# Masked attention of the last four head pairs: the selection mask is added to the position table on GpSimd, and VectorE makes these pairs' weights' low parts

## What is computed

```python
# forgetting attention (heads 0 to 7)
s = einsum('bqhd,bkhd->bhqk', q, k) * HEAD_DIM**-0.5 + F[t] - F[s]      # causal
p = softmax(s); out = p @ v
# sparse attention (heads 8 to 15)
iscore = sum_h w[t,h] * relu(q_idx[t,h] . k_idx[s]) ; causal
_, sel = lax.top_k(iscore, topk)                # topk = 128
logits = einsum(q, k[sel]) * HEAD_DIM**-0.5 + rel_bias[t5_bucket(t - sel)]
logits = where(valid, logits, -inf); p = softmax(logits); out = p @ v[sel]
merged = sigmoid(gate_fox) * (y_fox @ w_branch_fox) + sigmoid(gate_dsa) * (y_dsa @ w_branch_dsa)
```

## Time and profile before

| | us |
|---|---|
| three runs | 1383.68, 1383.83, 1384.71; median 1383.83 |
| profiled execution | 1383.52, span 1381.7 |
| busy: TensorE | 1358.7 (98%) |
| busy: VectorE, ScalarE, GpSimd | 809.0 (59%), 518.1 (37%), 560.1 (41%) |
| TensorE clock granted | 0.994 |

### The profile page before, as it was taken

How to read it: one execution, slowest core, us unless ns; L and a number is a source line. 1 busy time by engine, 2 the same in 40 slices (tenths; PEclk the granted TensorE clock), 3 DMA queues, 4 the chain that set the end, 5 groups by cost and what they waited for, 6 DMA issues and landing times.

```text
span 1381.7 us, 18469 instructions
## 1 busy us (share of the span) xinstructions
PE 1358.7 (98%) x6394; PEld 1105.6 (80%) x6398; DVE 809.0 (59%) x1082; ACT 518.1 (37%) x818; POOL 560.1 (41%) x230
## 2 busy tenths in 40 slices
PE   8999999999999999999999999999999999999997
PEld 6788878888888888886777777888878888888886
DVE  4565677574765757875888865344454243352474
ACT  5333224422323323235366665322345223142233
POOL 4333434454453635324322223444425535354361
PEclk9999999999999999989999999999999999999999
DMA  7222245373665645504423133332523423224221
GB/s 247 84 80 80 85 130 156 107 213 107 198 179 154 195 124 166 163 28 131 76 77 87 52 97 88 94 105 76 153 61 107 122 76 121 78 91 121 76 92 61
DMA packets 213236, 156.68 MB, mean 113 GB/s; under 512 B 8980, under 2 KB 193680, under 8 KB 213048
## 3 DMA queue, kind: packets, MB, share of 16 engines
q1 hardware_dynamic: 212856, 155.67, 38.6%
q10 hardware_dynamic: 320, 0.22, 0.1%
HBM read 153.73 MB, written 4.74 MB: 115 GB/s over the span
## 4 chain that ended last, share of the span: by engine, by line
PE 90%; issue 3%; POOL 2%; DVE 2%; DMA 2%; ACT 1%; ACTq 0%; DVEq 0%; POOLq 0%
PE ps L565 61%; PE ps L1034 12%; PE ps L922 3%; PE ps L983 3%; POOL w_lo L528 2%; PE ps L688 2%; PE ps L899 1%; PE ps L886 1%; DMA bias_rows<-bias_rows 1%; PE ps L872 1%; PE ps L813 1%; PE ps L873 1%; PE ps L663 1%; PE ps L651 1%; ACT w_hi L1081 0%
## 5 line engine op out<-in xcount | busy, mean ns | idle before, releaser
L528 POOL TENSOR_TENSOR w_lo<-raw,w_hi 128x1024 fp32r<-128x1024 f32 x222 | 557.0, 2517 | 789.5 <-ACT w_hi L1081 789.4
L565 PE MATMUL ps<-u_hi,w_hi 128*128 128x512 f32 x984 | 395.5, 402 | 3.5 <-POOL w_lo L528 1.8
L565 PE MATMUL ps<-u_hi,w_lo 128*128 128x512 f32 x984 | 384.8, 391 | 0.0
L565 PE MATMUL ps<-u_lo,w_hi 128*128 128x512 f32 x984 | 384.5, 391 | 0.0
L1081 ACT ACTIVATE w_hi<-raw 128x1024 fp32r<-128x1024 f32 x222 | 233.0, 1053 | 283.0 <-PE ps L1034 91.0
L565 PEld LDWEIGHTS ps<-u_hi,w_hi 128*128 128x128 f32 x984 | 186.4, 189 | 42.3 <-POOL w_lo L528 3.8
L565 PEld LDWEIGHTS ps<-u_hi,w_lo 128*128 128x128 f32 x984 | 185.4, 188 | 39.7
L565 PEld LDWEIGHTS ps<-u_lo,w_hi 128*128 128x128 f32 x984 | 185.8, 189 | 36.7 <-issue 1.0
L565 PE MATMUL ps<-y_hi,w_hi 128*128 128x512 f32 x320 | 126.7, 396 | 0.2
L565 PE MATMUL ps<-y_lo,w_hi 128*128 128x512 f32 x320 | 124.6, 389 | 0.0
L565 PE MATMUL ps<-y_hi,w_lo 128*128 128x512 f32 x320 | 124.6, 389 | 0.0
(11 more groups left out here) (270 smaller groups left out, 1816.0 us busy)
## 6 DMA issues: line engine op xcount, KB each, us to landing
raw<-w_in SPq DMA_DIRECT2D x69, 512.0 KB, 3.8
raw<-w_mlp SPq DMA_DIRECT2D x64, 512.0 KB, 3.9
adaw<-w_ada SPq DMA_DIRECT2D x32, 768.0 KB, 4.6
raw<-w_up SPq DMA_DIRECT2D x32, 512.0 KB, 6.6
raw<-w_down SPq DMA_DIRECT2D x32, 512.0 KB, 6.6
raw<-w_out SPq DMA_DIRECT2D x16, 512.0 KB, 4.4
bias_rows<-bias_rows SPq DMA_DIRECT2D x4, 635.0 KB
xtok<-x SPq DMA_DIRECT2D x4, 512.0 KB, 7.9
```

The costliest lines, as they stand in the source:

```text
L528: pool.tensor_tensor(w_lo[:, s, :], raw[:, s, :], w_hi[:, s, :], ALU.subtract).then_inc(lo_ready[s], 1)
L565: last = pe.matmul(ps[0:cols, bank, :], w[:, s, c], r[:, k, :], start=(k == ks[0] and w is w_hi and r is r_hi), stop=(k == ks[-1] and w is ...
```

## The change

- Pairs 4 to 7: TensorE's third matmul of each tile (876) goes. In its place GpSimd writes table plus mask into the tile's `prob(n)`, once the transposes of the tile that used the buffer before are through, and VectorE's `logits` waits for that and takes `prob(n)` as its second input.
- GpSimd no longer makes the low parts of both slots of `st_att` blocks 6 and 7 and of the first two `st_bra` blocks. VectorE makes these eight, at n = 0 (slot 0) and n = 3 (slot 1) of pairs 4 to 7.
- ScalarE's two casts stand earlier in all pairs: the one of slot 1 before `turned_odd(p, 1)` and `coming_exp(p, 3)`, the one of slot 0 before `turned_odd(p, 3)` and `coming_exp(p, 7)`.

```diff
@@ gpsimd
+            def masked_table(p, n):
+
+                i, tile = n // 2, 8 * p + n
+                keys = (i + 1) * P
+                pool.wait_ge(sem("tab_in"), 16 * (p + 1))
+                pool.wait_ge(sem("sel_ready"), i + 1)
+                pool.wait_ge(sem("att_t"), tile + 1 - LOOK)
+                pool.tensor_tensor(prob(n), tab2[:, 2 * (p % 2) + n % 2, T - keys:T], sel[:, i, 0:keys], ALU.add
+                                   ).then_inc(sem("masks"), 1)
...
-                if st is st_bra:
-                    for s, m in bra_order:
+                if st is st_att:
+                    with pool.Fori(0, NQ + 2) as i:
+                        for s in range(st.k):
+                            lo(st, s, i)
+                    for n in range(8 * NQ):
+                        masked_table(NQ + n // 8, n % 8)
+                elif st is st_bra:
+                    for s, m in bra_order[4:]:
                         lo(st_bra, s, m)
@@ tensor, s_step
-                pe.matmul(ps[:, bank, 0:keys], q_dn[:, at, q], k_both[:, at, 0:keys], start=False, stop=False)
-                if p >= NQ:
-                    pe.wait_ge(sem("sel_ready"), i + 1)
-                    last = pe.matmul(ps[:, bank, 0:keys], identb[:], sel[:, i, 0:keys], start=False, stop=True)
-                else:
+                last = pe.matmul(ps[:, bank, 0:keys], q_dn[:, at, q], k_both[:, at, 0:keys], start=False, stop=(p >= NQ))
+                if p < NQ:
                     last = pe.matmul(ps[:, bank, keys - P:keys], identb[:], causalb[:], start=False, stop=True)
@@ scalar, loop over the pairs
+                if p + 1 < 2 * NQ:
+                    ahead(st_att, 1, p + 1)
                 turned_odd(p, 1)
                 coming_exp(p, 3)
-                if p + 1 < 2 * NQ:
-                    ahead(st_att, 1, p + 1)
-                else:
+                if p + 1 == 2 * NQ:
                     cast(st_bra, 1, 1)
                     cast(st_bra, 2, 0)
...
-                turned_odd(p, 3)
-                coming_exp(p, 7)
                 if p + 2 < 2 * NQ:
                     ahead(st_att, 0, p + 2)
                 else:
                     cast(st_bra, 0, p + 3 - 2 * NQ)
+                turned_odd(p, 3)
+                coming_exp(p, 7)
@@ vector
-                    tab = tab2[:, 2 * (p % 2) + n % 2, T - keys:T]
+                    tab = prob(n)
+                    dve.wait_ge(sem("masks"), 3 + 8 * (p - NQ) + n + 1)
...
+            def w_low(s, g):
+
+                st, i = (st_att, g) if g < 2 * NQ else (st_bra, g - 2 * NQ)
+                dve.wait_ge(hi_ready[s], st.turn(s, i) + 1)
+                dve.tensor_tensor(w_lo[:, s, :], raw[:, s, :], w_hi[:, s, :], ALU.subtract).then_inc(lo_ready[s], 1)
...
                     coming_logits(p, n)
+                    if p >= NQ and n in (0, 3):
+                        w_low(n // 3, p + 2)
```

## The result

| | median of 5 runs, us | range |
|---|---|---|
| before | 1384.71 | 1383.68 to 1385.71 |
| after | 1392.55 | 1389.88 to 1393.95 |

The ratio is 1.0057, 95% interval 1.0042 to 1.0071: the change costs 7.8 us. The profiled execution of the changed kernel has a span of 1390.4 and a granted TensorE clock of 0.990. Busy times are 1357.9 for TensorE (before 1358.7), 821.7 for VectorE (809.0) and 568.1 for GpSimd (560.1). TensorE has 4.8 us less to do and is busy for 0.8 less, which is a first hint that the matmuls that are left ran slower somewhere.

The account below looks back on a forecast made before the run. TensorE and a loop through VectorE and ScalarE bind with nearly the same period. Terms 2.7 + 0 + 0.8 + 2.3 + 3.2 = 9.0 us on 1383.52, median 0.3 above: 1392.8; own range 1388 to 1397, 8 in 10 1382.5 to 1397.

Parts of the forecast that it names:

- the loop: Path through VectorE and ScalarE from one pair's first score matmul to the next, ending in k_lows; 0.1 to 0.3 us left.
- what shortens TensorE alone gains nothing: Attention stretch: the 4.8 us of mask matmuls taken off TensorE save no time while the loop stays.
- Casts earlier, +2.7: Pairs 1 to 3: earlier slot 0 cast makes divisions wait for GpSimd's low part; 0.9 us late each, +2.7 us.
- the earlier slot 1 cast falls in idle time of ScalarE: nothing: Pairs 1 to 3: moving the slot 1 cast earlier on ScalarE costs nothing.
- Pair 4, 0: Pair 4: division free of GpSimd's low part but starts 1.05 us later; logits 5 unmoved within 0.3, so 0.
- Pair 5, +0.8: Pair 5: w_low ahead of logits 5 and mask 5 share access in turn; logits 5 from 13.8 to 14.7, +0.8 us.
- Pair 6, +2.3: Pair 6: blocked final_norm, later exponentials, divisions and w_low running into masks delay logits 5; +1.1 to +3.5, taken +2.3 us.
- mask 2 falls on the second: it waits 0.7: Tail ahead of pair 6's logits 5: mask 2 blocks the second final_norm, which waits 0.7 us.
- Last stretch, +3.2: Pair 7 to tile 6's transposes: late logits 7, w_low(1) waiting for its cast, blocked division; +2.6 to +3.9, taken +3.2 us.
- Dear masks: Rival, last four stretches: 16-bit input doubles GpSimd's mask time, about 4 x 1.3 us on top, 1398; chance 0.08.
- Columns bind after all: Rival, attention stretch: VectorE's idle time takes in everything, TensorE's 4.8 to 5.3 us go, 1378.8; chance 0.12.
- Only the cast's place costs: Rival: masks and w_low slip into idle time in pairs 4 to 7; pairs 1 to 3 lose 2.7, 1386.5; chance 0.16.

Follow-up runs that it names:

- e2: Kernel before with the mask matmuls of pairs 4 to 7 left out, so the selection isn't applied: 1382.32 us, ratio 0.9983.
- e9: Changed kernel with masked tables in spare slots, w_low, y_lows and final_norm later, slot 0 cast early from pair 3 on only: 1381.20 us, ratio 0.9974.
- e10: Kernel before with y_lows and final_norm later and the slot 0 cast early from pair 3 on; masks stay on TensorE: 1383.60 us, ratio 0.9991.
- e1: Kernel before with only ScalarE's two weight casts of each pair one step earlier: 1386.57 us, ratio 1.0012.
- e12: Changed kernel with only the low part of st_bra block 1 moved behind the last pair's last division and turned_even: 1388.06 us, ratio 1.0021.
- e11: Changed kernel with w_low moved: slot 0 behind logits 5, st_bra block 1 behind the last pair's last division: 1388.21 us, ratio 1.0026.
- e8: Kernel before with only y_lows and final_norm moved behind k_lows and logits 7: 1383.66 us, ratio 0.9989.
- e4: Changed kernel with GpSimd writing the masked tables to four spare slots instead of the buffer of the probabilities: 1387.72 us, ratio 1.0019.
- e3: Changed kernel with ScalarE's old order of casts: 1395.58 us, ratio 1.0081.
- e5: e4 with ScalarE's old order of casts and GpSimd making all low parts between the masks: 1387.81 us, ratio 1.0019.
- e7: Changed kernel with only y_lows and final_norm moved behind k_lows and logits 7: 1391.45 us, ratio 1.0043.

## Why the prediction was right

The forecast was 1392.8, the median is 1392.55. That nearness is in part luck: the sum was +9.0 and the medians show +7.8, but the kernel before had a median of 1383.83 when the forecast was made and 1384.71 beside the changed kernel. (The bounds named for the forecast's own range add up to about 1389 to 1396, not 1388 to 1397.) The windows show +7.9. Point by point:

**TensorE and the loop have nearly the same period, and the 4.8 us appear nowhere.** True of the changed kernel: in pairs 4 to 6 the chain has gaps of 1.18, 1.72 and 1.72 us ahead of the first score matmul. But "what shortens TensorE alone gains nothing" was too strong: e2 gained 2.6. I had taken the place of the loop's end as fixed, but the loop holds score matmuls too, so it should get shorter with them (not tested by itself), and the last stretch has no `k_lows`. And e9 against e10 shows that half as much as the 4.8 can be had.

**Casts earlier, +2.7.** Right in mechanism (longer divisions in pairs 1 to 3, seen in the changed kernel and in e1), mis-sized: 1.92. And the three pairs aren't alike: 1.10, 0.42 and 0.40. In pair 2 logits 5 comes 14.07 us after the window's start, before 13.64 (746.28 less 732.64), so 0.4 later and not 0.9. Two readings differ from the forecast. GpSimd's low part ends 12.95 after the start, where I had 13.1, and the blocked division ends 0.40 behind it, where I had 0.65 (it takes 1.52, where I wrote 2 and more). The reciprocal moved by 0.5 (11.13 to 11.63), less than my 0.7, since it had waited for `q_lows` and not for the exponentials; but the division behind it was blocked until 747.50 in any case, so this made no difference. In pair 1 another step failed, "the earlier slot 1 cast falls in idle time of ScalarE: nothing". It did fall in idle time, but GpSimd's low part followed it forward onto a division, and that is the other 0.6 to 0.7 there.

**Pair 4, 0.** -0.39. Logits 5 starts where it did, as forecast (14.88 after the window's start, before 14.98); the rest of the pair is shorter. In e1 the early cast gives 0.80 there; with masks and `w_low` 0.4 of it is left.

**Pair 5, +0.8.** 0.72. Right, the mechanism too: logits 5 waits 0.95 for mask 5, which `w_low` had made 0.65 longer, and starts 14.55 after the edge (forecast 14.7).

**Pair 6, +2.3.** 2.24, and the wrong reasons: here the agreement is luck. `final_norm` in its tail was not blocked (0.75 us), so the step "mask 2 falls on the second: it waits 0.7" failed. What is there is pair 5's lateness again, about 0.7, and 1.5 us at the lower clock behind a gap of 1.72. In e12 both came again, to 0.03 us (22.14; gap 1.71; clock 0.53 from 817 to 819); in e11, with a gap of 1.25 and a clock of 1.00, the second did not.

**Last stretch, +3.2.** 3.44. The order of events is as forecast, and with it the rule of the Trainium skill (SBUF — State Buffer, Who interferes with whom) that issue order decides who waits for a whole instruction: `w_low` waits for the cast, GpSimd's low part of slot 2 takes the next turn, the division is blocked; `turned_even` is done 7.09 after logits 7's start (forecast 7.6). But logits 7 itself was only 0.2 late against its edge (18.63 us after the pair's first score matmul, before 18.42), not 0.8 to 2.0. So the path to the transposes of tile 6, which is what the term was for, grew by 1.86 and not by 3.2 (25.87, before 24.01), and 1.6 us of lower clock behind it made up for the rest. e12 shows that the whole term hangs on this one wait, and that it hid a gain of 1.24 besides.

**Prices.** A mask of 512 columns took 1.17 (taken 1.29), `w_low` 1.21 to 1.28 (1.25). "Dear masks" is out. The Trainium skill (GPSIMD Engine Reference, Performance versus the Vector engine) puts the cost of two inputs on the one read port that they share in turn. The trace shows the mask 0.12 under the 32-bit row, so an estimate by that rule was near, a little on the dear side. Whether the narrower input makes the 0.12 isn't shown, as the row is of a subtraction with another output type.

**Rivals.** "Columns bind after all" holds for the last stretch of e2 and of e12 and for e8 and e10, where TensorE has no gap, not for the change; in e9 TensorE works 18.67 of the 19.59 us of pair 5. "Only the cast's place costs" fell: e1 is +1.7, the change +7.8. What the prediction missed as a whole is the clock. Late masks and the late `w_low` open gaps of TensorE, and behind two of them it ran at half speed. Put at a place where they need not wait for the transposes (e4), the same instructions cost 5.3 us less in the windows: about 2.2 are the waits, 3.1 the clock.

So the terms were too large by 0.8 for the casts, 0.4 for pair 4, 0.1 for pair 5, 1.6 for pair 6 and 1.3 for the last stretch, 4.2 in all, and a clock effect of 3.1 us that was in none of them made most of it up. The forecast is nearer than its reasons deserve.

Open: why the gap of 1.72 us at 835.93 was not followed by the lower clock while the equal one at 813.82 was, in two kernels alike (e12 has 1.70 and 1.71). In e3, too, one of two nearly equal gaps was followed by it. These are its windows behind a gap of 1.82 and behind one of 1.89:

```profile
817.75:820.00 2.25, 2.25 (x17) 1.73 (x19) 0.70 (x2) 1.35 (x3) 0.00 (x0) 1.00 0.14 19
839.51:843.00 3.49, 3.48 (x21) 2.40 (x21) 1.48 (x3) 1.76 (x3) 0.00 (x0) 0.71 0.03 5
```

Open, too, is what of pair 5's and 6's 0.7 is `w_low` and what the masks: e4 moves the masks alone and takes pair 5 to 0.1 under the kernel before, e11 moves `w_low` alone and makes pair 5 longer by 0.39, so the masks' place matters more there, but no run has both moved and nothing else.

## What to carry to other kernels

Work moved off a full engine gains only if its result comes early enough: look first whether it can have a buffer of its own, so that it doesn't wait for the reader of the old one. That alone isn't enough: e5 has such buffers and is 2.8 us slower than before, since low parts and masks in a row block VectorE's divisions. In an engine that works in a fixed order, look for an instruction with a late input in front of one whose input is ready; here one such pair cost 4.7 us for 1.2 us of work, a third of it by the clock of the engine that was left waiting. And when a change is slower, test its parts: here its costs could be found one by one, and without them the idea was worth 2.4 us.

## What the hardware showed that was not expected

- TensorE's clock was at its lower level behind a standstill of 1.72 us: 0.50 from 817 to 819, back at 1.00 from 821. In the attention stretch of all these kernels, gaps of 1.71 (e12), 1.72, 1.89 (e3), 2.20 (e5), 2.79 (e7), 2.92 and 2.93 us (e3) were followed by it; gaps of 1.70 (e12), 1.72, 1.80 (e4) and 1.82 us (e3), and all of 1.31 or less, were not. So between 1.7 and 1.9 us the length of the gap alone didn't decide. The two falls of the changed kernel cost about 1.5 us each.
- A GpSimd addition of a 32-bit table and a 16-bit mask took 0.43, 0.68, 0.92 and 1.17 us for 128, 256, 384 and 512 columns: 0.19 plus 0.19 per 100 columns, where the nearest 32-bit subtraction took 1.29 for 512.
- Short GpSimd instructions in a row blocked VectorE as a long one does: in e5 the division of two tiles of 384 columns took 2.32 us from 830.47, beside four masks alone (830.16 to 833.46), where it takes 0.75 unblocked.
